# Gate tiles of feature tiles 2 to 7 taken in pairs, as 2x2 block products with seven products in place of eight, with x reloaded from DRAM

## The reference, cut to what matters

```
proj = einsum('bsd,dc->bsc', rmsnorm(x, norm_g), w_in)   # gl: the last 3*1024 columns of proj
pb = einsum('nbsc,ncd->nbsd', ys, w_branch)              # 3 x (512 -> 1024)
gates = sigmoid(gl.reshape(B, S, 3, 1024))
merged = einsum('bsnd,nbsd->bsd', gates, pb)
return x + einsum('bsd,de->bse', merged, w_out)
```

## Time and profile before

| | us |
|---|---|
| median of 3 executions | 2316.14 (2315.35 to 2316.17) |
| span of the profiled execution | 2314.2 |
| PE busy in that span | 2303.5 |
| DVE, ACT busy | 1481.9, 977.7 |

### The profile page before, as it was taken

One profiled execution on the slowest core, in us unless ns is written; L12 is line 12 of the kernel. 1 busy time (PEld: TensorE's weight loads), 2 busy tenths in 40 slices (PEclk: granted clock), 3 DMA queues, 4 the chain that ended last, 5 costly groups with the idle time before them and its releaser, 6 DMA issues.

```text
span 2314.2 us, 30125 instructions
## 1 busy us (share of the span) xinstructions
PE 2303.5 (100%) x11440; PEld 1881.8 (81%) x11440; DVE 1481.9 (64%) x2785; ACT 977.7 (42%) x1810; POOL 0.2 (0%) x4
## 2 busy tenths in 40 slices
PE   9999999999999999999999999999999999999998
PEld 7888888888888888888877788888887768888887
DVE  6788764345578774344577668566567767668565
ACT  5456542223446553222566533133236664323222
POOL 0000000000000000000000000000000000000000
PEclk9999999999999999999999999999999999999999
DMA  5333343332243333333231132314313113422312
GB/s 175 108 106 105 98 98 113 96 106 86 91 116 105 105 94 117 99 99 110 66 87 55 65 130 91 128 58 143 122 34 97 56 46 101 146 83 91 129 66 98
DMA packets 74766, 226.78 MB, mean 98 GB/s; under 512 B 15296, under 2 KB 16192, under 8 KB 73856
## 3 DMA queue, kind: packets, MB, share of 16 engines
q1 hardware_dynamic: 74480, 224.60, 31.4%
q10 hardware_dynamic: 144, 0.26, 0.0%
HBM read 205.29 MB, written 2.10 MB: 90 GB/s over the span
## 4 chain that ended last, share of the span: by engine, by line
PE 98%; DVE 1%; ACT 0%; DMA 0%; issue 0%; SPq 0%; DVEq 0%
PE bank L591 26%; PE bank L593 26%; PE bank L592 26%; PE bank L2239 2%; PE bank L2238 2%; PE bank L2240 2%; PE bank L1309 2%; PE bank L2055 1%; PE bank L2014 1%; PE bank L1293 1%; PE bank L2039 1%; PE bank L525 1%; PE bank L1282 1%; PE bank L1280 1%; PE bank L2068 1%; PE bank L2097 0%
## 5 line engine op out<-in xcount | busy, mean ns | idle before, releaser
L591 PE MATMUL bank<-h_hi,w_hi 128*128 128x512 f32 x1984 | 785.4, 396 | 0.2
L593 PE MATMUL bank<-h_lo,w_hi 128*128 128x512 f32 x1984 | 774.1, 390 | 0.0
L592 PE MATMUL bank<-h_hi,w_lo 128*128 128x512 f32 x1984 | 773.9, 390 | 0.0
L591 PEld LDWEIGHTS bank<-h_hi,w_hi 128*128 128x128 f32 x1984 | 373.1, 188 | 81.9 <-issue 7.6
L593 PEld LDWEIGHTS bank<-h_lo,w_hi 128*128 128x128 f32 x1984 | 372.7, 188 | 78.7
L1157 DVE TENSOR_TENSOR w_lo<-raw_w,w_hi 128x1024 fp32r<-128x1024 f32 x314 | 379.0, 1222 | 87.9 <-ACT w_hi L1145 84.5
L592 PEld LDWEIGHTS bank<-h_hi,w_lo 128*128 128x128 f32 x1984 | 373.4, 188 | 71.8
L1145 ACT ACTIVATE w_hi<-raw_w 128x1024 fp32r<-128x1024 f32 x313 | 326.7, 1055 | 156.0 <-DMA raw_w<-w_dram 155.6
L2475 ACT ACTIVATE nrm<-bank 128x512 f32<-128x512 f32 x44 | 26.3, 599 | 290.2 <-PE bank L593 290.2
L1609 ACT ACTIVATE ext<-bank 128x512 f32<-128x512 f32 x48 | 28.7, 598 | 275.1 <-PE bank L593 275.1
L1919 DVE TENSOR_TENSOR rope_a<-ext,bank 128x512 f32<-128x512 f32 x32 | 22.0, 688 | 165.8 <-PE bank L593 109.8
(11 more groups left out here) (374 smaller groups left out, 3502.4 us busy)
## 6 DMA issues: line engine op xcount, KB each, us to landing
raw_w<-w_dram SPq DMA_DIRECT2D x312, 512.0 KB, 3.6
down_raw<-w_dram SPq DMA_DIRECT2D x36, 512.0 KB, 4.4
extra_raw<-w_dram SPq DMA_DIRECT2D x10, 512.0 KB, 4.6
k_lo<-k_lo SPq DMA_DIRECT2D x32, 128.0 KB, 2.3
ln_row<-row_dram SPq DMA_DIRECT2D x4, 1024.0 KB, 6.7
last_raw<-w_dram SPq DMA_DIRECT2D x8, 512.0 KB, 4.8
x<-x_dram SPq DMA_DIRECT2D x4, 512.0 KB, 6.4
rowp<-row_dram SPq DMA_DIRECT2D x2, 1024.0 KB, 11.4
```

The costliest lines, as they stand in the source:

```text
L591: nc.tensor.matmul(dst, lh, rh, start=start, stop=False)
L592: nc.tensor.matmul(dst, ll, rh, start=False, stop=False)
L593: return nc.tensor.matmul(dst, lh, rl, start=False, stop=stop)
```

## The change

For the feature tiles 0 and 1 nothing changes. Feature tiles 2 to 7 are taken in three pairs (m, m+1), each with three branches: nine steps a layer, 18 in all. In a step, the two gate tiles (256 features by 512 tokens, contraction over 1024) are a 2x2 block product. The blocks are two halves of the contraction (4 tiles of 128 each), two feature tiles, and two halves of the tokens (256 columns each). The seven products of Winograd's form take the place of eight. Each product is 4 contraction tiles x 3 matmuls with 256 moving columns.

Around them:

- DVE builds four combinations of the activations once a layer (`combo_sums`, 8 operations of 128x1024, in the places of `rowp` and x). ACT rounds them (`combo_high`), DVE takes the remainder (`combo_low`).
- In each step DVE builds the weight combinations (`pair_sum`, `whole_sum`: 4 operations of 128x512), ACT rounds them, DVE takes the remainders (`sums_rest`, `whole_rest`). The projection weights get a buffer of their own (`proj_raw`, `proj_high`, `proj_rest`); they are no longer in the ring.
- Products accumulate on each other in the banks X, T and R. ACT copies X (three times) and T (once) out between products (`product_copy`), DVE makes three combinations of 128x256, ACT applies the sigmoids, and DVE multiplies, adds and writes `mrg_hi` and `mrg_lo` (`merge_tile`).
- x, whose place holds combinations, is read again from DRAM: in layer 0 from the input, in layer 1 from `x_keep`, where SP writes it early in that layer. `rowp`, `gain_row` and the mask `swa` are loaded later than before.

The core of the difference (helpers for slots and piecewise loads left out):

```diff
+        PAIR_SEVEN = ((0, PAIR_X), (4, PAIR_T), (5, PAIR_X), (2, PAIR_R), (1, PAIR_X), (6, PAIR_T), (3, PAIR_X))
...
+            def load_proj(n):
+                sp.wait_ge(unit_done, n - 2 if STEP_OF[n][1] else n - 4)
...
+                        if n == n0 + B1_OUT + 3:
+                            sp.wait_ge(unit_done, n0 + B1_OUT - 1)
+                            bring_x(stage)
...
+            def pair_products(s):
...
+                for q, (a, bank) in enumerate(PAIR_SEVEN):
+                    if q == 0:
+                        split_wait(pe, n)
+                        if turn:
+                            pe.wait_ge(sig_ready, 2 * turn - 1)
+                    elif q == 1:
+                        pe.wait_ge(sum_split, 2 * turn + 1)
...
+                    elif q == 2:
+                        pe.wait_ge(product_copied, 4 * turn + 1)
...
+                    elif q == 4:
+                        split_wait(pe, n + 1)
+                        pe.wait_ge(product_copied, 4 * turn + 3)
+                    elif q == 5:
+                        pe.wait_ge(product_copied, 4 * turn + 2)
+                    elif q == 6:
+                        pe.wait_ge(sum_split, 2 * turn + 2)
+                        pe.wait_ge(product_copied, 4 * turn + 4)
+                    if s == 0 and a in COMBO_ORDER:
+                        pe.wait_ge(combo_ready, at(combo_ready, COMBO_ORDER.index(a) + 1))
...
+                    for k in range(4):
...
+                        nc.tensor.matmul(to, high[:, w], m_hi, start=begin, stop=False, skip_group_check=True)
+                        nc.tensor.matmul(to, low[:, w], m_hi, start=False, stop=False, skip_group_check=True)
+                        made = nc.tensor.matmul(to, high[:, w], m_lo, start=False, stop=k == 3, skip_group_check=True)
...
+            def proj_high(s):
+                turn = PAIR_STEPS * layer + s
+                act.wait_ge(proj_loaded, 32 * (turn + 1))
...
+            combo_high(6)
+            act.wait_ge(tile_out[1], at(tile_out[1], before1(B1_GATE) + 3 * PLAIN_MM))
+            for s in range(PAIR_STEPS):
...
+                product_copy(turn, 1, 1, ext[2][:, FIRST_HALF], PAIR_X)
+                cast_to(act, n + 3)
+                product_copy(turn, 2, 2, ext[3][:, SECOND_HALF], PAIR_T)
+                product_copy(turn, 3, 3, ext[3][:, FIRST_HALF], PAIR_X)
+                proj_high(s)
+                if more:
+                    cast_to(act, n + 4)
+                product_copy(turn, 4, 4, ext[2][:, SECOND_HALF], PAIR_X)
...
-            for mm in range(KD):
+            for mm in range(PLAIN_MM):
...
+                    if (mm, i) == (0, 1):
+                        combo_sums()
+                    elif (mm, i) == (1, 0):
+                        combo_low(1)
+                        combo_low(5)
+                    elif (mm, i) == (1, 1):
+                        pair_sum(0)
+                        whole_sum(0)
+                        split_to(dve, n0 + B1_PAIR)
+                        sums_rest(0)
+                        combo_low(4)
+                        split_to(dve, n0 + B1_PAIR + 1)
+                        whole_rest(0)
+                        combo_low(6)
+                merge_out(mm, total)
+            for s in range(PAIR_STEPS):
...
+                if s:
+                    whole_rest(s)
+                if more:
+                    pair_sum(s + 1)
...
+                if more:
+                    whole_sum(s + 1)
+                    sums_rest(s + 1)
+                    split_to(dve, n + 3)
+                merge_tile(s, 0)
+                if more:
+                    split_to(dve, n + 4)
+                merge_tile(s, 1)
             split_to(dve, n0 + B1_OUT + 5)
```

More of the change, by code:

```diff
@@ L55 @@
 GATE_TURN = 4
+PLAIN_MM = 2
+B1_PAIR = B1_GATE + 9
+PAIR_STEPS = 9
 B1_OUT = 80
@@ L421, in program @@
         LAST_OF = {first_unit(DEPTH + layer) + B2_LAST + i: (layer, i) for layer in range(DEPTH) for i in range(LAST_UNITS)}
-        RING = [n for n in range(UNITS) if n not in EXTRA and n not in LAST_OF]
+        STEP_OF = {first_unit(layer) + B1_PAIR + 3 * s + j: (layer, s, j)
+                   for layer in range(DEPTH) for s in range(PAIR_STEPS) for j in range(3)}
+        PROJ_UNITS = [n for n in STEP_OF if STEP_OF[n][2] == 2]
+        RING = [n for n in range(UNITS) if n not in EXTRA and n not in LAST_OF and n not in PROJ_UNITS]
         TURN = {n: r for r, n in enumerate(RING)}
@@ L450, in down_stored, with pair_of, pieces @@
             return first_unit(DEPTH) + layer * B2_STORED + at + 1
+        def pair_of(s):
+            return PLAIN_MM + 2 * (s // 3), s % 3
+        def pieces(n):
+            if n not in STEP_OF:
+                return [(stored_at(n), 0, 0, UNIT)]
+            layer, s, j = STEP_OF[n]
+            m, i = pair_of(s)
+            if j < 2:
+                wanted = [(gate_at(m + j, i), KD)]
+            else:
+                wanted = [(gate_at(m + half, i) + KD, 4) for half in range(2)]
+            out, to = [], 0
+            for first, tiles in wanted:
+                while tiles:
+                    unit, c = divmod(first, KD)
+                    take = min(tiles, KD - c)
+                    out.append((first_unit(layer) + B1_GATE + unit, c * P, to * P, take * P))
+                    first, tiles, to = first + take, tiles - take, to + take
+            return out
         def loaded_parts(n):
-            return sum(2 if m in KR_UNITS else 1 for m in RING[TURN[n] % RAW:TURN[n] + 1:RAW])
+            return sum(2 if m in KR_UNITS else len(pieces(m)) for m in RING[TURN[n] % RAW:TURN[n] + 1:RAW])
         def slot_of(n, ring, extra, last):
@@ L1333, in gate @@
             def gate(mm, i, ks=range(KD), ends=True):
-                gate_tile(gate_at(mm, i), gate_bank(mm, i), ks, KD, h_hi, h_lo, ends)
+                return gate_tile(gate_at(mm, i), gate_bank(mm, i), ks, KD, h_hi, h_lo, ends)
             def project(mm, i):
@@ L1399, in tensor_block1 @@
             project(0, 2)
-            for mm in range(1, KD):
+            for mm in range(1, PLAIN_MM):
                 for i in range(3):
@@ new lines, in whole_rest, with proj_rest @@
+            def whole_rest(s):
+                dve.wait_ge(sum_cast, 2 * (PAIR_STEPS * layer + s) + 2)
+                nc.vector.tensor_tensor(whole_lo[:, :], whole_raw[:, :], whole_hi[:, :].bitcast(F32), ALU.subtract).then_inc(sum_split, 1)
+            def proj_rest(s):
+                dve.wait_ge(proj_cast, PAIR_STEPS * layer + s + 1)
+                for j in range(2):
+                    cols = slice(SEQ * j, SEQ * (j + 1))
+                    made = nc.vector.tensor_tensor(proj_lo[:, cols], proj_raw[:, cols], proj_hi[j][:, :].bitcast(F32), ALU.subtract)
+                made.then_inc(proj_split, 1)
@@ L1923, in vector_block1 @@
                         st.wait(st(nc.vector.tensor_tensor(total, total, term, ALU.add)))
[L1924 to L1930 removed]
+                    split_to(dve, min(n0 + B1_GATE + gate_units(gate_at(mm, i), KD) + 2, n0 + B1_PAIR - 1))
```

275 lines of the change are left out of this document (257 added, 18 removed).

## The result

The changed kernel takes **2322.95 us** (median of 5 runs, 2322.56 to 2326.05) against 2316.07 us (2315.35 to 2316.17) for the kernel before: ratio 1.0033, 95% interval 1.0021 to 1.0046. It is slower by 6.9 us. Forecast were 2318.0 us, with a range of 2311 to 2327. The profiled execution took 2322.56 us with a span of 2320.8 us, 6.6 us more than the 2314.2 us of before.

What follows compares the result with a forecast made beforehand. PE was taken to bound the kernel, busy 2303.5 of 2314.2 us. The sum -14.4 + 2 x (3.9 + 4.2) = +1.8 us gave span 2316.0 and median 2318 us, range 2311 to 2327.

Steps and rivals of the forecast that it cites:

- no change: Whole kernel: time within 0.2% of before, 2311.5 to 2320.8 us; chance 56%.
- The forecast's case: Whole kernel: matmul saving against waits at layer starts and ends, span +1.8 us, median 2318 us; chance 58%.
- PE's clock falls in the long waits: Rival, layer-end waits: half clock adds 2.3 us per wait, twice, giving 2322.6 us; chance 10%.
- Gain, 14.4 us: Pair steps: 84 narrow matmuls replace 48 wide ones, saving 0.80 us a step over 18 steps.
- Steady steps, no wait: Pair steps after the layer start: PE never waits for ACT, DVE or SP; a step lasts 15.5 us.
- The late hand-over in every step: Rival, each step: late projection loads delay product 6, 18 x 0.5 = 9 us, giving 2327; chance 17%.
- Layer start, 3.9 us: Step 0: PE waits for first split, combination 4 and ACT's first copy; 3.9 us a layer, bounds 2 and 6.
- Layer end, 4.2 us: Output projection's start: PE waits for its split behind both merges; 4.2 us a layer, bounds 3.8 and 4.6.
- The rest at nothing: Reload of x, later small loads and writing `x_keep`: 0 to 4 us in all, taken as 0.
- The granted clock is 1.00 behind the waits: Sign to check: after the layer-start and layer-end waits PE still runs at full clock, 2.4 GHz.

Runs made afterwards that it cites:

- the last experiment: Changed kernel with the layer-end split ahead of the merges, first-step combinations one gate tile earlier, and step 0's fifth product copied before the cast: 2301.74 us.
- the experiment with the reload alone: Kernel before, plus only writing x to DRAM in the second layer and loading it back in both layers: 2316.40 us, ratio 1.0002.
- the kernel with the end repaired: Changed kernel with the output projection's first split made before the pair's merges in each layer's last step: 2310.93 us.
- the one with the end filled: Changed kernel with 16 extra unread 128x512 matmuls in the wait at each layer's end: 2319.74 us.
- the kernels with the start repaired: Changed kernel with first-step combinations one gate tile earlier: 2317.07 us; also with the layer-end split before the merges: 2303.39; also with the fifth product copied first: 2301.74.

## Why the prediction was right, and where it fell short

The time lay in the range and the verdict, slower, was the one with 34%, not the 56% of "no change". The forecast's case was 5 us too low, and the rival "PE's clock falls in the long waits", to which 10% were given, gave 2322.6. So the range held the result by its width: the case on which it was centred left out a term of 4.7 us.

- **Gain, 14.4 us: right.** Narrow pace 0.120 as read from another place of the trace; 15.54 us a step against 15.52; and the last experiment returns 14.2 us once nothing is given back. The estimate of 21.4 us by the Trainium skill (TensorE: Matmul & The Clock Gate, section Back-to-back issue gap) would have been 7 us too much.
- **Steady steps, no wait: right.** The 84 narrow starts of the step shown are at pace, and no wait behind step 0 is listed. The late hand-over in every step (17%) did not come.
- **Layer start, 3.9 us: 3.7.** The three waits stand where they were put, the last one 2.3 us instead of 2.5. A fourth (0.8 to 1.0 us, product 6) was hidden behind these three, since with PE later the copy was in time; the steady-state account of that hand-over, spare 0.8 us, did not hold for step 0, where ACT's cast waits for DVE's sum.
- **Layer end, 4.2 us: 4.4.** Right in its place and cause; undoing it alone gives 12.0 us back.
- **The rest at nothing: right**, by the experiment with the reload alone. (The changed kernel without the reload was not tried.)
- **"The granted clock is 1.00 behind the waits": wrong.** This is the step that failed. It was argued from one stretch behind the kernel's last matmul, where full clock was still granted after 4.6 us, and so a 4.2 us wait was thought to be borne. It wasn't: in the three profiles that have end waits of 4.4 to 4.9 us left idle, all six were followed by half clock. The one reading didn't bound the rest: from the last matmul's end to the fall of the clock the profiles show from 2.0 to 5.3 us. The rival's size was right by two errors: it priced 2.3 us for each end wait (measured 1.6), and had none for the start waits, of which one cost 1.5. That an idle gap between bursts of matmuls can bring the half clock back is what the Trainium skill says (TensorE: Matmul & The Clock Gate, section Why this matters for your kernels). The trace agrees, with 1.6 us of half clock beside a wait of 4.4.

The spread of the changed kernel's runs (3.5 us) has the same origin, as far as the medians of the experiments can tell: it falls to 0.6 us when the waits are filled, and to 0.3 us when they are gone. Why the start wait of 2.3 us is followed by half clock in one layer and not in another stays open.

## What to carry to other kernels

A saving on the engine that bounds can be worked out from the pace that the narrower form shows elsewhere in the trace; what decided here is what the other engines must have ready at the two ends of the new loop. A split that the old code made ahead of the last tile's merging must stay ahead of it. An idle stretch of TensorE can cost more than its length: each wait of 4.4 us or more here cost 1.5 to 2.4 us on top, and so did some of those of 2.3 us. Where such a wait can't be removed, matmuls whose result nobody reads are cheaper than silence.

## What the runs showed of the hardware

- Waits of 4.4 to 4.9 us before a matmul, in which TensorE was left idle, were followed by a granted clock of 0.50 six times out of six (three profiles). Waits of 2.3 us were followed by it in four of six places (the changed kernel's layer 1 of its two, both of the kernel with the end repaired, layer 1 of the one with the end filled); each of these stood behind two shorter ones, of 0.3 and 0.8 us, within some 6 us, and no run tells it apart from them. Where the only wait was one of 1.0 us or less (both starts of the kernels with the start repaired) it was never followed by it.
- The clock fell from 2.0 us (the kernel with the start repaired, layer 0's end) to 5.3 us (the changed kernel, the same place) after the end of the last matmul ahead of the wait, so in some places during the wait and in others after work had begun again.
- A fall cost 1.5 to 2.4 us, whatever was running: wide matmuls at 0.427 us apart instead of 0.2267, narrow at 0.213 instead of 0.120. Full clock was back 3.1 to 5.0 us after TensorE resumed work.
- 16 matmuls of 128x512 in a wait of 4.4 us kept the clock at 1.00, in both layers.
- 4 MB more moved by DMA (2 MB read, 2 MB written) beside a busy TensorE changed nothing: the stretch took 401.87 us with them and 401.86 without.
